# One row operation behind each of eight feed-forward pairs, and an earlier place for the prologue's rows

## The chip, the cores and the metric

The kernel runs on one core of a Trainium2 chip. The metric is the device time of one execution in microseconds. A core has TensorE (PE, the matrix engine; its weight loads are shown apart as PEld), VectorE (DVE), ScalarE (ACT), GpSimd (POOL) and SyncE (SP, which here issues almost all DMAs). The engines run side by side and wait for one another by semaphores.

## The reference

One layer of a decoder trunk, on 2048 rows of 1024 values, in float32:

```python
mem_n = rms_norm(mem, mem_norm)
h = rms_norm(x, mix_pre_norm)
z = h @ w_in                       # split into pool, conformer, gated-conv parts
y = concat([pool_mixer(...), conformer_conv(...), short_gated_conv(...)]) @ w_out
x = x + rms_norm(y, mix_post_norm)
h = rms_norm(x, xattn_pre_norm)
y = cross_attention(h, mem_n, wq, wk, wv, wo)      # 4 heads, 256 memory tokens
x = x + rms_norm(y, xattn_post_norm)
h = rms_norm(x, ffn_pre_norm)
u = causal_dwconv(h @ ffn_w_up, ffn_conv_w)        # 3 taps, 5632 channels
gate, val = split(u)
x = x + rms_norm((silu(gate) * val) @ ffn_w_down, ffn_post_norm)
```

`rms_norm(x, g)` is `x * rsqrt(mean(x*x) + 1e-6) * g`, row by row.

## The kernel before

**Tiles and phases.** The rows are worked through in four tiles of 512. Phases follow each other: a prologue (PREP), the mixers for four tiles (MIX_FIRST, MIX twice, MIX_LAST), attention for four tiles (ATT_FIRST, ATTN), the feed-forward for four tiles (FFN). Every operand of a matmul is split into a high and a low part, and each product is three matmuls (lines 1546 to 1548).

**Weight slots.** Weights go through TensorE in slots of 128 x 1024 values, 24 matmuls each. SyncE loads a slot into one of four `raw` buffers, ten slots ahead at most. ScalarE rounds it into the high half of one of four `pair` buffers (`hi`, L676), three slots ahead of TensorE; GpSimd subtracts that from the raw values for the low half (`lo`, L644). The order of ScalarE's instructions is written out by hand: within a slot's step, `hi` for the slot three places on stands in front of the work on this slot's result.

**Banks.** Results of column slots go in turn through four PSUM banks, `colb`. The list of items of a phase (`PREP_ITEMS`, and `PREP_HIS` for the part that is rounded) gives each item its bank by its place, so an item waits until the item four places before it has been read out. ScalarE writes the rounded value (L685), VectorE the low part (L1093, or L1095 with a gain), and the latter frees the bank.

**Prologue.** TensorE transposes the memory rows (8 items), multiplies them with eight slots for the keys and eight for the values (256 columns per matmul), transposes the pooling maps (`bd`), waits for `h_ready`, and transposes the scaled rows of the first tile, two of eight items behind each of the last four value slots. Between memory transposes and the first key slot stands `banks_ready`, which waits for all. ScalarE sums the squares of the rows; VectorE computes the inverse root `rh` in pieces between the key roundings and scales the four row blocks `xh` (`first_row`, L1132) behind the first four values. Then six convolution slots follow, whose results VectorE uses in three 31-tap convolutions (L1238), and two pooled slots. SyncE stores keys and values to DRAM and, at the end of the prologue, loads the keys of head 0 back (`load_head`).

**First mixer tile.** TensorE needs these keys in `a_rows(0)`. Later it waits for VectorE with the transposes of the next rows: for `h_ready`, and for banks that VectorE frees in `sconv_chunk` (L1307).

**Feed-forward.** A tile has two halves. Each half runs 22 column slots, that is 11 pairs of a gate and a value slot, and 11 row slots into `accb`. For pair j, ScalarE issues `hi` of slot 2j+3, copies the result of slot 2j (L995), issues `hi` of slot 2j+4 and copies slot 2j+1. VectorE (`ffn_pair`) fetches two columns of the halo (L1384), multiplies by the taps (L1393 twice, L1396 four times), stores the halo (L1399); ScalarE does the silu (L998); VectorE multiplies (L1401); ScalarE rounds (L1000); VectorE subtracts (L1201), and that ends the pair. With the end of a pair, ScalarE comes to `hi` of slot 2j+5.

**End of a tile.** `new_rows` adds the normed result to the rows of x: for each of four row blocks a multiply by root and gain (L1176, 1024 columns) and an addition (L1179, the last one L1183). At the last attention tile and the feed-forward tiles but the last, it is interleaved with the first pairs of the next tile by `between`. `LEAD = RB` (4) says how many pairs are done there; the loop over the rest starts at that number:

```python
for r in range(RB):
    if between is not None and r:
        between(r - 1)
    step(nc.vector.scalar_tensor_tensor(y[:, r, :], ..., gain[:, :], ...))
    if r:
        settle(1)
        nc.vector.tensor_tensor(xt[:, r - 1, :], ..., ALU.add)
```

With the last addition x is new (`x_new`). SyncE waits for that at place `ROWS_AT` of its loop over a tile's slots, stores the rows, loads the gain, and two places on the next rows `xt`. ScalarE waits for it before it writes the next result of the row slots.

## Time and profile before

| | |
|---|---|
| median of three timed runs | 2629.49 us |
| the three runs | 2623.81, 2632.18, 2629.49 us |
| the profiled execution | 2624.15 us |
| its span, first to last instruction | 2622.0 us |
| mean granted TensorE clock | 0.989 |

| engine | busy us | share |
|---|---|---|
| TensorE (PE) | 2541.6 | 97% |
| weight loads (PEld) | 2113.0 | 81% |
| VectorE (DVE) | 1514.3 | 58% |
| ScalarE (ACT) | 915.7 | 35% |
| GpSimd (POOL) | 846.1 | 32% |

A row of the timeline has the start in us from the span's start, the duration in us, engine, line, operation, output and input by the program's names, and a count where consecutive instructions were merged; in brackets stands the engine's idle time before the row and what ended it. Matmuls are pipelined, so their rows overlap: the distance from start to start is the pace. The granted clock of 1.00 is TensorE at full speed.

### The profile page before, as it was taken

What the parts mean: (1) busy time and instruction counts of PE and PEld (TensorE: products, weight loads), DVE (VectorE), ACT (ScalarE), POOL (GpSimd) and SP (SyncE); (2) the same over time, 40 slices, a digit from 0 to 9 for tenths busy, and PEclk for the clock granted to TensorE, in tenths of its full rate; (3) what the DMA queues carried; (4) which work ended last, traced back from release to release, by engine and by line L of the source; (5) the groups of instructions that cost most, each with busy time, mean ns of one, the idle gap of its engine ahead of it and who ended that gap; (6) DMA issues with size and microseconds to landing.
All of it is one profiled execution on the core that took longest, in us unless ns stands there. A gap on an engine that the chain in (4) does not pass through costs nothing.

```text
span 2622.0 us, 32632 instructions
## 1 busy us (share of the span) xinstructions
PE 2541.6 (97%) x11713; PEld 2113.0 (81%) x11713; DVE 1514.3 (58%) x2452; ACT 915.7 (35%) x1515; POOL 846.1 (32%) x346
## 2 busy tenths in 40 slices
PE   7999899999999999999999999999999999999997
PEld 6787788878787888887888878888878888878886
DVE  5698877877744532557436276256385264672462
ACT  4433322233334333333333333333334233333332
POOL 6431200000023000034534444444445444445342
PEclk9999999999999999999999999999999999999999
DMA  8796684856868757744333334323354332353331
GB/s 252 250 336 234 209 310 153 299 202 218 290 238 310 301 212 258 268 147 159 113 88 97 95 115 163 117 82 100 92 163 136 94 91 89 90 168 112 89 96 64
DMA packets 313817, 452.62 MB, mean 173 GB/s; under 512 B 12073, under 2 KB 234558, under 8 KB 292670
## 3 DMA queue, kind: packets, MB, share of 16 engines
q1 hardware_dynamic: 305101, 438.56, 49.3%
q10 hardware_dynamic: 8560, 12.06, 1.4%
q8 instruction: 89, 1.46, 0.2%
q14 instruction: 67, 0.54, 0.1%
HBM read 368.78 MB, written 81.79 MB: 172 GB/s over the span
## 4 chain that ended last, share of the span: by engine, by line
PE 82%; DVE 11%; issue 3%; ACT 2%; DMA 1%; SPq 0%; ACTq 0%; DVEq 0%
PE colb L1546 16%; PE colb L1547 16%; PE colb L1548 16%; PE accb L1546 11%; PE accb L1547 11%; PE accb L1548 11%; PE colb L1583 2%; DVE accb L1238 2%; DVE arena L1384 1%; DVE arena L1396 1%; DVE xt L1179 1%; PE accb L1750 1%; DVE arena L1176 1%; DMA raw<-in_xattn_wq 1%; DMA kept<-pair 0%
## 5 line engine op out<-in xcount | busy, mean ns | idle before, releaser
L644 POOL TENSOR_TENSOR pair<-raw,pair 128x1024 fp32r<-128x1024 f32 x339 | 845.2, 2509 | 1748.2 <-ACT pair L676 1737.8
L1546 PE MATMUL colb<-hT,pair 128*128 128x512 f32 x1952 | 765.2, 392 | 16.8 <-issue 12.7
L1547 PE MATMUL colb<-hT,pair 128*128 128x512 f32 x1952 | 763.0, 391 | 0.0
L1548 PE MATMUL colb<-hT,pair 128*128 128x512 f32 x1952 | 762.7, 391 | 0.0
L676 ACT ACTIVATE pair<-raw 128x1024 fp32r<-128x1024 f32 x339 | 355.5, 1052 | 472.6 <-PE accb L1548 277.7
L1546 PE MATMUL accb<-pair,act 128*128 128x512 f32 x1120 | 440.4, 393 | 11.7 <-issue 4.8
L1546 PEld LDWEIGHTS colb<-hT,pair 128*128 128x128 f32 x1952 | 368.7, 189 | 99.0 <-issue 22.5
L1547 PE MATMUL accb<-pair,act 128*128 128x512 f32 x1120 | 437.8, 391 | 0.0
L1548 PE MATMUL accb<-pair,act 128*128 128x512 f32 x1120 | 437.6, 391 | 0.0
L1548 PEld LDWEIGHTS colb<-hT,pair 128*128 128x128 f32 x1952 | 368.4, 189 | 77.3
L1547 PEld LDWEIGHTS colb<-hT,pair 128*128 128x128 f32 x1952 | 368.4, 189 | 75.5
L1393 DVE TENSOR_SCALAR arena<-arena,par 128x512 f32<-128x512 f32 x176 | 219.2, 1286 | 348.3 <-ACT arena L995 347.2
L1546 PEld LDWEIGHTS accb<-pair,act 128*128 128x128 f32 x1120 | 211.2, 189 | 60.4 <-issue 11.3
L1548 PEld LDWEIGHTS accb<-pair,act 128*128 128x128 f32 x1120 | 211.4, 189 | 44.6
L1547 PEld LDWEIGHTS accb<-pair,act 128*128 128x128 f32 x1120 | 211.5, 189 | 42.8
L998 ACT ACTIVATE arena<-arena 128x512 f32<-128x512 f32 x88 | 55.6, 632 | 544.0 <-DVE arena L1399 544.0
L1396 DVE SCALAR_TENSOR_TENSOR arena<-arena,par 128x512 f32<-128x512 f32 x352 | 240.1, 741 | 0.0
L1238 DVE SCALAR_TENSOR_TENSOR arena<-arena,par 128x512 f32<-128x512 f32 x261 | 184.7, 784 | 0.0
L1201 DVE TENSOR_TENSOR act<-arena,act 128x512 fp32r<-128x512 f32 x120 | 88.4, 737 | 82.5 <-ACT act L1000 61.5
L995 ACT ACTIVATE arena<-colb 128x512 f32<-128x512 f32 x176 | 103.0, 585 | 61.6 <-PE colb L1548 61.5
L1165 DVE TENSOR_TENSOR small<-small 128x4 f32<-128x4 f32 x12 | 2.0, 163 | 192.6 <-ACT junk L697 192.6
L1509 DVE TENSOR_TENSOR arena<-arena,accb 128x512 f32<-128x512 f32 x32 | 21.8, 688 | 135.2 <-PE accb L1548 135.2
(162 smaller groups left out, 2421.4 us busy)
## 6 DMA issues: line engine op xcount, KB each, us to landing
pair<-kept SPq DMA_DIRECT2D x123, 1024.0 KB, 5.0
raw<-in_ffn_w_up SPq DMA_DIRECT2D x176, 512.0 KB, 3.8
raw<-in_ffn_w_down SPq DMA_DIRECT2D x176, 256.0 KB, 2.9
kept<-pair SPq DMA_DIRECT2D x41, 1024.0 KB, 7.0
raw<-in_w_in SPq DMA_DIRECT2D x17, 512.0 KB, 6.7
xh<-in_x SPq DMA_DIRECT2D x4, 2048.0 KB, 15.3
xt<-in_x SPq DMA_DIRECT2D x4, 2048.0 KB, 15.5
x_mixed<-xt SPq DMA_DIRECT2D x4, 2048.0 KB, 11.2
```

What stands on the lines that cost most here:

```text
L644: nc.gpsimd.tensor_tensor(pair[:, b, 1, :], raw[:, r, :], pair[:, b, 0, :].bitcast(F32), ALU.subtract).then_inc(lo_done, 1)
L676: nc.scalar.activation(pair[:, b, 0, :], raw[:, r, :], ACT.Copy).then_inc(hi_done, 1)
L995: nc.scalar.activation(uf[:, j % 2, e, HS:LS], colb[bank_of(FFN, c)][:, :], ACT.Copy)\
L998: nc.scalar.activation(cv[:, 0, :], cv[:, 0, :], ACT.Silu).then_inc(silu_done, 1)
L1201: nc.vector.tensor_tensor(dst, src, hi.bitcast(F32), ALU.subtract).then_inc(lo_written, 1)
L1238: step(nc.vector.scalar_tensor_tensor(total, src, w, sums[k % 2], ALU.mult, ALU.add))
L1393: step(nc.vector.tensor_scalar(cv[:, e, :], u[:, e, k:k + T], w, None, ALU.mult))
L1396: step(nc.vector.scalar_tensor_tensor(cv[:, e, :], u[:, e, k:k + T], w, cv[:, e, :], ALU.mult, ALU.add))
L1546: nc.tensor.matmul(dst, sh, mh, start=first, stop=False)
L1547: nc.tensor.matmul(dst, sh, ml, start=False, stop=False)
L1548: return nc.tensor.matmul(dst, sl, mh, start=False, stop=last)
L1583: ins = nc.tensor.transpose(dst[:, n * P:(n + 1) * P], src, ident[:, :])
```

## The change

In `new_rows` with `between`, eight pairs of the next tile are done instead of four: pair 0, multiply of row block 0, pair 1, addition of row block 0, pair 2, multiply of block 1, and so on, to the addition of block 3 behind pair 7. The multiply that stood ahead of pair 0 stands behind it. `LEAD` becomes 8 and `ROWS_AT` of the feed-forward 14.

In the prologue, the transposes of the pooling maps stand behind the second value slot instead of the fourth, the row transposes behind value slots 4 to 7 instead of 5 to 8 (counted from 1), and the eighth value slot behind them all. ScalarE scales the row blocks, two behind each of the first two values, after a wait for the new semaphore `root_ready`. The first key slot waits for each memory value by itself. SyncE's `load_head(sp, 0, 0)` stands behind the last convolution slot's place in its loop.

```diff
-    PREP_HIS = [("mem", k) for k in range(KD)] + [("k", i) for i in range(KD)] + [("v", i) for i in range(KD // 2)] + [("bd",)] +\
-               sum([[("v", KD // 2 + i), ("row", 2 * i), ("row", 2 * i + 1)] for i in range(KD // 2)], [])
+    V_ROWS = KD // 2 - 1
+    PREP_HIS = [("mem", k) for k in range(KD)] + [("k", i) for i in range(KD)] + [("v", 0), ("v", 1), ("bd",), ("v", 2)] +\
+               sum([[("v", V_ROWS + i), ("row", 2 * i), ("row", 2 * i + 1)] for i in range(KD // 2)], []) + [("v", KD - 1)]
@@ SyncE
+                    elif what == "c" and k == CSLOTS - 1:
+                        sp.wait_ge(kv_stored, 16 * 2 * HEADS)
+                        load_head(sp, 0, 0)
                     elif what == "pooled":
...
                         if k == 1:
-                            sp.wait_ge(kv_stored, 16 * 2 * HEADS)
-                            load_head(sp, 0, 0)
-            ROWS_AT = {MIX_FIRST: 0, MIX: 0, MIX_LAST: 0, ATT_FIRST: 0, ATTN: 0, FFN: 8}
+            ROWS_AT = {MIX_FIRST: 0, MIX: 0, MIX_LAST: 0, ATT_FIRST: 0, ATTN: 0, FFN: 14}
@@ ScalarE
                 key_values(1, i)
-                if i == KD // 2 - 1:
+                if i == 0:
+                    sc.wait_ge(root_ready, 1)
+                if i < 2:
+                    for r in (2 * i, 2 * i + 1):
+                        scaled = nc.scalar.activation(xh[:, r, :], xh[:, r, :], ACT.Copy, scale=rh[:, r:r + 1])
+                if i == 1:
+                    scaled.then_inc(h_ready, 1)
                     sc.wait_ge(xp_full, xp_at(PREP, 0, ("bd",)) + 1)
...
@@ VectorE
-            LEAD = RB
+            LEAD = 2 * RB
...
+            ve.sem_inc(root_ready, 1)
             for i in range(KD):
                 key_values(1, i)
-                if i < RB - 1:
-                    first_row(i)
-                elif i == RB - 1:
-                    first_row(i).then_inc(h_ready, 1)
-                if i == KD // 2 - 1:
+                if i == 1:
                     ve.wait_ge(hi_written, PREP_HIS.index(("bd",)) + 1)
...
+                if between is not None:
+                    for r in range(RB):
+                        between(2 * r)
+                        step(nc.vector.scalar_tensor_tensor(y[:, r, :], y[:, r, :], rs[:, r:r + 1], gain[:, :], ALU.mult, ALU.mult))
+                        between(2 * r + 1)
+                        settle()
+                        last = nc.vector.tensor_tensor(xt[:, r, :], xt[:, r, :], y[:, r, :], ALU.add)
+                    last.then_inc(x_new, 1)
+                    return
@@ TensorE
-            banks_ready(PREP, 0, item[PREP]["mem", 0], KD)
-            for i in range(KD):
+            first = split_ready(PREP, 0, place[PREP]["k", 0])
+            keys = bank_free(PREP, 0, item[PREP]["k", 0])[:, 0:M]
+            for k in range(KD):
+                i = item[PREP]["mem", k]
+                pe.wait_ge(col_free[bank_of(PREP, i)], uses_of(PREP, 0, i) + 1)
+                ins = products(keys, pieces(first, k * P, (k + 1) * P), (memT[:, 0, k, :], memT[:, 1, k, :]), k == 0, k == KD - 1)
+            ins.then_inc(slot_used, 1)
+            for i in range(1, KD):
                 column_slot(PREP, 0, place[PREP]["k", i], item[PREP]["k", i], memT, M)
             for i in range(KD):
                 column_slot(PREP, 0, place[PREP]["v", i], item[PREP]["v", i], memT, M)
-                if i == KD // 2 - 1:
+                if i == 1:
                     pe.wait_ge(maps_in, 16 * NW)
                     transposes(PREP, 0, item[PREP]["bd",], [bd[:, e, :] for e in range(NP_)]).then_inc(xp_full, 1)
+                if i == V_ROWS:
                     pe.wait_ge(h_ready, 2)
-                if i >= KD // 2:
-                    for k in range(2 * (i - KD // 2), 2 * (i - KD // 2) + 2):
+                if V_ROWS <= i < KD - 1:
+                    for k in range(2 * (i - V_ROWS), 2 * (i - V_ROWS) + 2):
                         head(PREP, 0, item[PREP]["row", k], k)
```

ScalarE's and VectorE's loops over the row items follow the same new order.

## Rows read from the trace of the kernel before

**Rows 1.** The page, busy us, share of the span and instructions of each engine.

```profile
PE 2541.6 (97%) x11713; PEld 2113.0 (81%) x11713; DVE 1514.3 (58%) x2452; ACT 915.7 (35%) x1515; POOL 846.1 (32%) x346
```

**Rows 2.** Timeline of TensorE, prologue: start, duration, line, idle before in brackets.

```profile
17.79 0.55 PE L1546 MATMUL colb<-act,pair 128*128 128x256 f32 x1 [2.00 <-DVE act L1095]
...
23.47 0.38 PE L1548 MATMUL colb<-act,pair 128*128 128x256 f32 x1
23.69 0.29 PE L1546 MATMUL colb<-act,pair 128*128 128x256 f32 x1
23.81 0.29 PE L1547 MATMUL colb<-act,pair 128*128 128x256 f32 x1
...
60.52 0.58 PE L1546 MATMUL colb<-act,pair 128*128 128x256 f32 x1 [5.12 <-DVE xh L1132]
...
65.30 1.04 PE L1583 MATMUL colb<-ident,xh 128*128 128x128 f32 x8
...
76.53 1.04 PE L1583 MATMUL colb<-ident,xh 128*128 128x128 f32 x8
...
79.62 0.47 PE L1546 MATMUL colb<-hT,pair 128*128 128x512 f32 x1 [2.05 <-DVE hT L1095]
```

**Rows 3.** Timeline of VectorE, prologue.

```profile
15.80 1.66 DVE L1095 SCALAR_TENSOR_TENSOR act<-colb,par,act 128x256 fp32r<-128x256 f32 x4 [0.83 <-ACT act L685]
...
48.30 2.11 DVE L1076 TENSOR_TENSOR small<-small 128x4 f32<-128x4 f32 x1
50.44 0.16 DVE L1077 SCALAR_TENSOR_TENSOR small<-small 128x4 f32<-128x4 f32 x1
...
51.17 2.77 DVE L1132 TENSOR_SCALAR xh<-xh,small 128x1024 f32<-128x1024 f32 x1
...
56.98 0.74 DVE L1132 TENSOR_SCALAR xh<-xh,small 128x1024 f32<-128x1024 f32 x1
```

**Rows 4.** Timelines of ScalarE and GpSimd, prologue.

```profile
46.85 1.05 ACT L676 ACTIVATE pair<-raw 128x1024 fp32r<-128x1024 f32 x1
...
47.98 2.40 POOL L644 TENSOR_TENSOR pair<-raw,pair 128x1024 fp32r<-128x1024 f32 x1 [0.47 <-ACT pair L676]
```

**Rows 5.** Timeline of TensorE, first mixer tile.

```profile
135.27 0.58 PE L1546 MATMUL accb<-act 128*128 128x256 f32 x1 [4.38 <-DMA act<-kvd]
...
211.20 0.95 PE L1583 MATMUL colb<-ident,xh 128*128 128x128 f32 x4 [1.96 <-DVE arena L1307]
```

**Rows 6.** Timeline of VectorE, first mixer tile.

```profile
210.45 0.69 DVE L1307 TENSOR_TENSOR arena<-arena,colb 128x512 f32<-128x512 f32 x1
```

**Rows 7.** Timeline of VectorE, first multiply of the first and fourth boundary.

```profile
1147.55 3.37 DVE L1176 SCALAR_TENSOR_TENSOR arena<-arena,small,gain 128x1024 f32<-128x1024 f32 x1
...
2254.72 1.29 DVE L1176 SCALAR_TENSOR_TENSOR arena<-arena,small,gain 128x1024 f32<-128x1024 f32 x1 [0.21 <-DVE small L1078]
```

**Rows 8.** Timeline of TensorE, third boundary: slots 9, 11 and 25 of the tile.

```profile
1925.02 0.47 PE L1546 MATMUL colb<-hT,pair 128*128 128x512 f32 x1 [0.85 <-issue]
...
1938.28 0.52 PE L1546 MATMUL colb<-hT,pair 128*128 128x512 f32 x1 [2.13 <-issue]
...
2016.65 0.47 PE L1546 MATMUL accb<-pair,act 128*128 128x512 f32 x1
```

**Rows 9.** Windows: stretch, its length, busy us by engine, clock, DMA share, GB/s.

```profile
1938.28:1949.16 10.88, 10.88 (x41) 8.85 (x42) 7.19 (x11) 4.13 (x6) 4.26 (x2) 0.84 0.34 97
```

**Rows 10.** Timeline of VectorE, third boundary: ends of pairs 0, 3, 4, 10.

```profile
1894.06 0.69 DVE L1201 TENSOR_TENSOR act<-arena,act 128x512 fp32r<-128x512 f32 x1 [0.70 <-ACT act L1000]
...
1922.60 3.40 DVE L1179 TENSOR_TENSOR xt<-xt,arena 128x1024 f32<-128x1024 f32 x1
...
1934.14 0.69 DVE L1201 TENSOR_TENSOR act<-arena,act 128x512 fp32r<-128x512 f32 x1 [0.70 <-ACT act L1000]
...
1946.13 0.69 DVE L1201 TENSOR_TENSOR act<-arena,act 128x512 fp32r<-128x512 f32 x1 [0.70 <-ACT act L1000]
...
2013.10 0.69 DVE L1201 TENSOR_TENSOR act<-arena,act 128x512 fp32r<-128x512 f32 x1 [0.70 <-ACT act L1000]
```

**Rows 11.** Timeline of GpSimd, third boundary, same time as the addition at 1922.60.

```profile
1921.79 3.13 POOL L644 TENSOR_TENSOR pair<-raw,pair 128x1024 fp32r<-128x1024 f32 x1 [6.88 <-ACT pair L676]
```

More of the change, by code:

```diff
@@ L1155, in _ @@
                     ins.then_inc(col_free[b], 1)
[L1156 to L1157 removed]
+                if V_ROWS <= i < KD - 1:
+                    for k in range(2 * (i - V_ROWS), 2 * (i - V_ROWS) + 2):
                         lo_item(PREP, 0, PREP_HIS.index(("row", k)), item[PREP]["row", k], hT[:, 1, k, :], hT[:, 0, k, :],
@@ L1172, in new_rows @@
                 ve.wait_ge(xt_in, step_tile.at(p, t, 1) * 16)
+                if between is not None:
[7 more added lines that the diff above has]
+                    return
                 for r in range(RB):
-                    if between is not None and r:
-                        between(r - 1)
                     step(nc.vector.scalar_tensor_tensor(y[:, r, :], y[:, r, :], rs[:, r:r + 1], gain[:, :], ALU.mult, ALU.mult))
@@ L1179, in new_rows @@
                         nc.vector.tensor_tensor(xt[:, r - 1, :], xt[:, r - 1, :], y[:, r - 1, :], ALU.add)
-                if between is not None:
-                    between(RB - 1)
                 settle()
```

9 lines of the change are left out of this document (3 added, 6 removed).

## The prediction

> **What bounds the kernel now.** I read the page's busy table first [rows 1]: TensorE is busy for 97% of the span, VectorE for 58%. So only what takes an idle or slow stretch away from TensorE can shorten the run. Then I listed TensorE's idle stretches in order of time and kept those that the diff can touch.
>
> Prologue [rows 2]: the first key slot starts at 17.79, right behind the eight memory transposes, because it waits for all eight roundings. At 60.52 TensorE has idled 5.12 us for the scaled rows of x, and the slot behind it takes 4.8 us, until the transposes at 65.30, where its neighbours take 2.7: it runs mostly at the lower of the clock's two levels (1.2 and 2.4 GHz); at 79.62 it idles another 2.05 us for the last transposed value's rounding. In the first mixer tile it idles 4.38 us at 135.27 for the keys' load and 1.96 us at 211.20 for VectorE [rows 5].
>
> Feed-forward: at the start of each of four tiles TensorE idles about 2.1 us (2.13 at 1938.28, the others alike) and then runs slow; the mean granted clock of the two slots behind it is 0.84 [rows 8, 9]. What holds it is a ring of three engines. VectorE ends a pair with the subtraction on L1201; only then does ScalarE round the weights of the slot five places on, GpSimd takes their low part, and TensorE may start. The slot at 1938.28 starts 4.14 us behind the subtraction at 1934.14; with no row operation between, the slot at 2016.65 starts 3.55 us behind 2013.10 [rows 8, 10]. That last pair, the eleventh, matters most: the slot that it releases starts as soon as it can, so TensorE has no reserve left there. The pace of the ring over eleven pairs, not the size of one idle stretch, decides how long a tile's first half takes.
>
> **Part by part. The first key slot.** Its 24 products now wait value by value. They share a bank with the fifth memory value, whose rounding is the first of the four that VectorE starts at 15.80 [rows 3]; four took 1.66 us, so the bank is free at about 16.3 instead of 17.79: 1.45 us sooner. The matmuls there start 0.21 us apart, and 0.12 us apart once the clock has risen, at 23.69 [rows 2]. If the rise stays where it is, 1.45 us of work moves into the slow stretch and 1.45 x 0.12/0.21 = 0.8 us is left. I take 1.2, bounds 0.8 and 1.5.
>
> **Scaled rows and transposes.** On VectorE the four row scalings start at 51.17 and take up to 2.77 us, the shortest 0.74 [rows 3]; they are interleaved with value roundings. The long ones overlap GpSimd's operations. ScalarE needs 1.05 us for 1024 columns, as its rounding at 46.85 shows [rows 4], and never has such a long one. ScalarE now waits for the root first. The root's last round was late because of GpSimd: the weights that ScalarE rounds at 46.85 set GpSimd going at 47.98, and VectorE's small multiply at 48.30 took 2.11 us instead of 0.16 [rows 3, 4]. In the new order these weights stand behind that wait, so this collision goes and the root is ready at about 49.0. Four scalings with one weight rounding and one value rounding between them: 49.0 + 4 x 1.05 + 1.05 + 0.4 = 54.7. TensorE, which now does the transposes of the pooling maps after the second value, ends the fourth at about 55.5. The wait of 5.12 is gone with 0.8 us to spare, and its clock loss with it, 4.8 less 2.7 (3.75 from one start of transposes to the next, less 1.04 for the transposes [rows 2]), so 2.1. The eighth value slot now covers the rounding of the last rows, which took the 2.05. Sum 5.12 + 2.1 + 2.05 = 9.2; I take 9.0, as two banks come free only just in time. Queued behind ScalarE's wait are the weights of the fifth value and the rounding of the second; both have over 3 us. If the root comes at 50.8 as before, the rows end 1.8 us later, 1.0 us too late, and the banks of the maps and of the third value, freed behind them, add 0.6 and 0.7 and a little more in the next slot: about 3 us lost, so the lower bound is 6.1.
>
> The Trainium skill speaks against this move: "ScalarE: Activation LUTs", Rules for kernel authors, says that multiplications belong on VectorE, not ScalarE. By it four scalings cost 4 x (1.05 - 0.74) = 1.2 us more, a little over the reserve worked out above, and the wait would stay with 0.4 us. The durations of up to 2.77 us in [rows 3] show why I do not follow it here.
>
> **The keys' load on SyncE's queue** moves in front of one weight load, one stored slot and four stores of pooled rows, all of which are issued one DMA's issue time later. That removes the 4.38 us at 135.27. I cost it at nothing: from the last convolution slot on, VectorE is busy with hardly a gap until L1307 at 210.45, and TensorE waits for exactly that at 211.20 [rows 5, 6]. TensorE only arrives there earlier. Hence also: what the prologue saves up to the last convolution slot moves this whole VectorE chain, and reaches 211. Bounds 0 and 2, since VectorE has two short idles of its own.
>
> **Row operations.** Before, four rounds hold two row operations each, then (after the first pair) 1894.06 to 1934.14 is three rounds of 13.36 us, the next, with one last addition, takes 11.99, and the six up to 2013.10 take 11.16 [rows 10]; TensorE needs 10.88 (48 matmuls of 0.2267). The single row operation costs 0.83, because VectorE idles about 2.25 us in a bare round anyway and only GpSimd is held back. The second costs 1.37 more: the addition at 1922.60 took 3.40 us, waiting for GpSimd's 3.13 us subtraction [rows 10, 11]. After: eight rounds with one. Half hold an addition (11.99), half the multiply, 0.06 us longer (12.05): 96.2, and two bare ones 22.3, together 118.5. Before: 40.1 + 12.0 + 67.0 = 119.1. So each boundary gains 0.5. The idle stretches do change: instead of one of 2.1 with a slow clock, some five of up to 1.1. The slow clock cost nothing in the end, since TensorE caught up with the ring by the eleventh pair; so its going brings nothing. At two of the four boundaries the first multiply stands on the path ahead of pair 0: at 1147.55 it ends the wait for GpSimd, at 2254.72 nothing else is late [rows 7]; there pair 0 starts about 1.1 and 1.0 sooner. At the other two VectorE waits some 4 us for the slot itself. Sum 4 x 0.5 + 2.1 = 4.1. Bounds: if the multiply does not hold GpSimd back, its rounds take 11.5, and four boundaries gain 4 x 4 x 0.55 = 9 more; if each row operation costs half of what two do, (13.36 - 11.16)/2 = 1.1, eight rounds are 98.1 and a boundary loses 1.3, which with the two earlier starts makes 2.1 - 5.2 = -3.
>
> A rule of the Trainium skill on this: "SBUF — State Buffer", Who interferes with whom, says that a VectorE instruction with two SBUF inputs and a GpSimd instruction that reads SBUF exclude each other for the whole instruction. The 3.40 and 3.13 us of [rows 10, 11] agree; without exclusion the multiply's rounds would be the 11.5.
>
> The second store of rows, the gain and the next load of rows move on SyncE from place 8 to place 14. x is new behind pair 7, about 1894 + 7 x 12 + 2.5 = 1980.5; SyncE comes to place 14 when GpSimd has done slot 20, at about 1984. It does not wait, and the weight loads queued behind it have four buffers. Cost nothing.
>
> **Sum.** 1.2 + 9.0 + 0 + 4.1 = 14.3 us. The profiled execution took 2624.15 (span 2622.0), and would take 2609.9. The three timed runs have a median of 2629.49, 5.3 above it: predicted 2629.5 - 14.3 = 2615.2.
>
> **Rivals.** (a) The root is as late as before: prologue 7.3, total 11.4, 2618. For it: VectorE's other small operations there also take 2.3 us. Against: the colliding GpSimd operation can't start. Chance 0.15. (b) The price of a row operation is 1.1: total 10.2 - 3.1 = 7.1, 2622. Against it stands the 11.99. Chance 0.1. (c) The prologue's gain is lost in the first mixer tile, where transfers are dense: VectorE's chain meets more of GpSimd's operations, each costing 2.3 us, and TensorE's longer idle ahead of 211 keeps the clock low longer. Half the 10.2 goes, total 9 or less, about 2622. Chance 0.15. (d) Slower: with 1.1 us of idle in each of five slot pairs, the clock falls to 1.2 GHz in the feed-forward start. A fall for nine matmuls costs 1.8 us and is swallowed by the next idle stretches. It decides the result once it lasts for a whole pair, 48 x 0.2 = 9.6 us less 1.1 of idle, 34 us over four tiles: 2649. For it: behind 2.1 us the clock fell. Against: behind the 0.85 us at 1925.02 it did not [rows 8]. Chance 0.04. (e) The multiply does not hold GpSimd back: 23 saved, 2606. Chance 0.08. (f) The load move does not do what it is for, its transfer being slowed by its neighbours: same time as forecast, since it is off the path.
>
> **Chances.** Forecast 0.48, the others as given. The range 2606 to 2623 takes in (a), (b), (c) and (e) and leaves out (d) and the ends of the rest. Measurement tells about 0.3%, 7.9 us. Faster: the forecast, (a), (e) and a third of (b) and (c), less a little for the scatter of the medians: 0.75. Same 0.21, slower 0.04.
>
> **What would show it.** Right: no idle of TensorE over 1 us between the fourth value slot and the first convolution slot, which starts near 69; VectorE's chain unbroken until the heads of the first mixer tile, TensorE idling there 5 us or more; first feed-forward rounds 12.0 apart on L1201, eight of them, the eleventh subtraction within 1 us of its old distance from the first. Wrong: rounds of 12.3 or 11.5; scaled rows later than the fourth value slot; a granted clock near 0.5 for more than 4 us in the feed-forward start.

## The result and the profile after

The changed kernel took 2610.64 us in the median of four runs (2609.72 to 2612.18), the kernel before 2630.08 (2623.81 to 2632.18) beside it: ratio 0.9932, interval 0.9914 to 0.9951. The profiled execution went from 2624.15 us to 2610.44, its span from 2622.0 to 2608.6, its mean granted clock from 0.989 to 0.995. Both medians and spans count here: the spans, which the steps below are read from, are 13.4 us apart, the medians 19.4, because the profiled execution of before was among its fastest.

The page of the changed kernel: busy time of the engines, which answers [rows 1].

```profile
PE 2532.9 (97%) x11713; PEld 2102.9 (81%) x11713; DVE 1534.2 (59%) x2448; ACT 919.9 (35%) x1519; POOL 841.4 (32%) x346
```

TensorE is 8.7 us less busy with the same matmuls: fewer of them ran at the lower clock. VectorE is busier although four scalings left it: an operation that is held up by GpSimd counts as busy, as a copy of 2.37 us further down shows.

TensorE's timeline of the changed kernel, prologue (start, duration, engine, line, operation; in brackets the idle time before and what ended it). It answers [rows 2].

```profile
16.75 0.55 PE L1554 MATMUL colb<-act,pair 128*128 128x256 f32 x1 [0.76 <-DVE act L1104]
...
53.57 1.06 PE L1591 MATMUL colb<-ident,xh 128*128 128x128 f32 x8
55.10 0.36 PE L1554 MATMUL colb<-act,pair 128*128 128x256 f32 x1 [0.47 <-DVE act L1102]
...
66.32 0.36 PE L1554 MATMUL colb<-act,pair 128*128 128x256 f32 x1
...
69.26 0.40 PE L1554 MATMUL colb<-hT,pair 128*128 128x512 f32 x1
...
105.84 0.47 PE L1554 MATMUL colb<-hT,pair 128*128 128x512 f32 x1 [1.03 <-POOL pair L647]
```

The idle stretches of 5.12 and 2.05 us are gone, the value slots run at the higher clock throughout, and the first convolution slot starts at 69.26. ScalarE and VectorE of the same stretch show why, against [rows 3, 4]:

```profile
47.03 0.17 DVE L1087 SCALAR_TENSOR_TENSOR small<-small 128x4 f32<-128x4 f32 x1
```

```profile
47.28 2.19 ACT L744 ACTIVATE xh<-xh,small 128x1024 f32<-128x1024 f32 x2 [1.98 <-DVEq L1147]
49.38 1.04 ACT L679 ACTIVATE pair<-raw 128x1024 fp32r<-128x1024 f32 x1
50.33 0.36 ACT L688 ACTIVATE act<-colb 128x256 fp32r<-128x256 f32 x1
50.59 2.18 ACT L744 ACTIVATE xh<-xh,small 128x1024 f32<-128x1024 f32 x2
```

The root is ready at 47.2 (its last small operation takes 0.17 us; one took 2.11 before), and two scalings take 2.19 us, so the rows are ready at 52.8, before the transposes behind the fourth value slot start at 53.57.

In the first mixer tile TensorE's waits, which answer [rows 5], are:

```profile
114.95 0.66 PE L1591 MATMUL colb<-ident,pair 128*128 128x128 f32 x4 [2.06 <-ACT arena L838]
152.47 1.53 PE L1717 MATMUL accb<-ident,arena 128*128 128x128 f32 x12 [1.93 <-DVE arena L1249]
182.32 0.47 PE L1554 MATMUL colb<-hT,pair 128*128 128x512 f32 x1 [1.11 <-DVE arena L1300]
189.67 0.47 PE L1554 MATMUL accb<-pair,act 128*128 128x512 f32 x1 [1.64 <-POOL pair L647]
199.06 0.66 PE L1591 MATMUL colb<-ident,xh 128*128 128x128 f32 x4 [1.96 <-DVE arena L1315]
```

And at the start of the first attention tile TensorE waits longer than before, and the clock falls behind it. The first row is that of the kernel before, the second that of the changed one. The window's columns are the stretch, its length, the busy time of PE, PEld, DVE, ACT and POOL, then the granted clock, the DMA share and GB/s.

```profile
822.60 1.97 PE L1750 MATMUL accb<-ident,xh 128*128 128x128 f32 x16 [1.93 <-DVE xh L1084]
```

```profile
809.63 3.62 PE L1766 MATMUL accb<-ident,xh 128*128 128x128 f32 x16 [4.07 <-DVE xh L1093]
```

```profile
809.63:813.63 4.00, 4.00 (x19) 3.92 (x20) 1.98 (x3) 2.41 (x4) 0.00 (x0) 0.57 0.88 364
```

VectorE's timeline at the start of a feed-forward tile, around pair 0 (answers [rows 7, 10]; L1209 is the subtraction that ends a pair, L1179 the multiply, L1182 the addition, L1392 a copy of 128x4):

```profile
1144.56 0.69 DVE L1209 TENSOR_TENSOR act<-arena,act 128x512 fp32r<-128x512 f32 x1 [0.70 <-ACT act L1009]
1145.17 1.27 DVE L1179 SCALAR_TENSOR_TENSOR arena<-arena,small,gain 128x1024 f32<-128x1024 f32 x1
1146.36 2.37 DVE L1392 COPY arena<-arena 128x4 f32<-128x4 f32 x1
...
1156.68 0.69 DVE L1209 TENSOR_TENSOR act<-arena,act 128x512 fp32r<-128x512 f32 x1 [0.70 <-ACT act L1009]
1157.29 1.22 DVE L1182 TENSOR_TENSOR xt<-xt,arena 128x1024 f32<-128x1024 f32 x1
```

A round with a row operation takes 12.12 us (multiply, as here from 1144.56 to 1156.68) or 12.05 (addition), a bare one, without such an operation, 11.16. The row operation itself is short. It pushes the 128x4 copy behind it against GpSimd's subtraction, and the copy stands 2.37 us. In a bare round VectorE waits 2.15 us for ScalarE at about that place, so most of the copy's time costs the round nothing.

At this boundary TensorE idles four times for about 0.9 us, where it idled twice for 2.29 and 2.21 before (at 1188.10 and 1201.45). The clock over the whole stretch is 1.00; before it was 0.98 over the like stretch from 1177 to 1257, and 0.84 over the 10.88 us of [rows 9] at the third boundary:

```profile
1197.13 0.47 PE L1554 MATMUL colb<-hT,pair 128*128 128x512 f32 x1 [0.96 <-issue]
1209.17 0.47 PE L1554 MATMUL colb<-hT,pair 128*128 128x512 f32 x1 [0.89 <-issue]
1221.27 0.47 PE L1554 MATMUL colb<-hT,pair 128*128 128x512 f32 x1 [0.94 <-issue]
1233.31 0.47 PE L1554 MATMUL colb<-hT,pair 128*128 128x512 f32 x1 [0.91 <-issue]
```

```profile
1165.00:1245.00 80.00, 76.08 (x331) 61.23 (x329) 67.01 (x75) 28.92 (x42) 35.54 (x14) 1.00 0.37 113
```

**Where the 13.4 us lie**, as the lead of the changed kernel's trace over the one before at the same place:

| place | lead, us | what came or went |
|---|---|---|
| first mixer slot (116.26 to 105.84) | 10.42 | prologue |
| heads of the first mixer tile (211.20 to 199.06) | 12.14 | VectorE's chain there is 1.7 shorter |
| first attention tile (822.60 to 809.63) | 12.97 | mixer tiles |
| pair 0 of the first feed-forward tile (1156.96 to 1144.56) | 12.40 | clock fall in the attention -1.7, earlier pair 0 +1.1 |
| its 11th pair (1276.26 to 1263.53) | 12.73 | rounds of the first boundary |
| pair 0 of the fourth and last tile (2261.94 to 2248.61) | 13.33 | second earlier pair 0, +0.9 |
| last pair (2558.21 to 2544.80) | 13.41 | |

The table compares one trace of each kernel, and not all of a lead is the change's. In two traces of the kernel before the first mixer slot starts at 116.26 and 115.17, in two of the changed kernel at 105.84 and 103.83: the prologue's gain lies between 9.3 and 12.4 us. From there to the attention the two traces of the changed kernel take 703.8 and 710.2 us, so the 2.55 us that the lead gains in the mixer tiles can't be given to the change.

### The profile page after: what moved, and what is told of

It is laid out like the page before. It is cut to its first block, busy times and chain, and to the rows that moved or that the text cites. A ratio compares the mean times of both kernels' runs of the same rounds, so it can differ in the third digit from the quotient of the medians.

```text
span 2608.6 us, 32631 instructions
## 1 busy us (share of the span) xinstructions
PE 2532.9 (97%) x11713; PEld 2102.9 (81%) x11713; DVE 1534.2 (59%) x2448; ACT 919.9 (35%) x1519; POOL 841.4 (32%) x346
## 4 chain that ended last, share of the span: by engine, by line
PE 90%; DVE 5%; issue 1%; DMA 1%; ACT 1%; SPq 0%; ACTq 0%; DVEq 0%
PE colb L1554 19%; PE colb L1556 18%; PE colb L1555 18%; PE accb L1554 11%; PE accb L1556 11%; PE accb L1555 11%; PE colb L1591 2%; DVE accb L1246 2%; PE accb L1766 1%; DMA raw<-in_xattn_wq 1%; DMA kept<-pair 0%; ACT junk L700 0%; DVE small L1086 0%; DVE small L1087 0%; DVE xh L1093 0%
## 5 line engine op out<-in xcount | busy, mean ns | idle before, releaser
L1401 DVE TENSOR_SCALAR arena<-arena,par 128x512 f32<-128x512 f32 x176 | 238.9, 1397 | 317.2 <-ACT arena L1004 315.2
L1209 DVE TENSOR_TENSOR act<-arena,act 128x512 fp32r<-128x512 f32 x120 | 87.6, 730 | 81.0 <-ACT act L1009 61.5
```

Of the source, the lines that this page charges most:

```text
L1209: nc.vector.tensor_tensor(dst, src, hi.bitcast(F32), ALU.subtract).then_inc(lo_written, 1)
L1401: step(nc.vector.tensor_scalar(cv[:, e, :], u[:, e, k:k + T], w, None, ALU.mult))
```

## The experiments

The line numbers of a kernel are its own. Spans in brackets are those of the profiled execution. The three groups of runs had medians of 2626.8, 2628.7 and 2627.5 us for the kernel before beside them; each ratio is to its own group.

### The unchanged kernel, traced again

> The kernel before, unchanged, for a second trace of it. Ratio 1.000. Theory A: a span and stage times within 1 us of the first trace. Theory B: a span 5 us longer than the first one's 2622.0, the extra in the feed-forward starts, and a mean granted clock under 0.989.

2627.46 us (2619.85 to 2632.11, 12 runs), ratio 1.0003, interval 0.9991 to 1.0016; [2621.5]. From pair 0 of the first feed-forward tile to the last pair it took 1401.30 us, the first trace 1401.25. The feed-forward part of these two traces is the same to 0.1 us; they differ ahead of it, by 1.1 us at the first mixer slot.

### The feed-forward part alone

Against the changed kernel:

```diff
-    V_ROWS = KD // 2 - 1
-    PREP_HIS = ... ("v", 0), ("v", 1), ("bd",), ("v", 2)] + ...
+    PREP_HIS = ... [("v", i) for i in range(KD // 2)] + [("bd",)] + ...
...
-                        scaled = nc.scalar.activation(xh[:, r, :], xh[:, r, :], ACT.Copy, scale=rh[:, r:r + 1])
...
-            first = split_ready(PREP, 0, place[PREP]["k", 0])
+            banks_ready(PREP, 0, item[PREP]["mem", 0], KD)
```

The prologue is the one of before, whole, and so is the place of the keys' load.

> The kernel before with the feed-forward part of the change alone (eight pairs, one row operation behind each, rows stored at place 14). Theory A, the ring of three engines sets the pace to the eleventh pair: eight rounds of 12.1 and two of 11.2 us, TensorE at the eleventh pair within 0.3 us of before in every tile but the two that start earlier, so 2 us faster, about 2628 where the kernel before has 2630. Theory B, the idle stretches of 2.1 us cost more in ordinary executions than in the profiled one of the kernel before, through the clock: 7 us faster, about 2623, with the spread of the runs under 3 us. No fall of the granted clock behind idles of 0.9 us either way.

2624.78 us (2616.77 to 2629.74, 11 runs), ratio 0.9993, interval 0.9982 to 1.0003; [2614.6]. From pair 0 to the last pair 1399.88, that is 1.4 less than before, where eight rounds of one row operation were to give 0.5 at each of four boundaries and the earlier start at the last one 1.0. With the 1.1 us of the earlier first pair 0 the part is worth some 2.5 us of 2627 by the traces; the medians say 2, with an interval that takes in nothing. Of its start the trace shows something else. Row of the unchanged kernel, traced again:

```profile
822.05 1.97 PE L1750 MATMUL accb<-ident,xh 128*128 128x128 f32 x16 [2.15 <-DVE xh L1084]
```

and of this kernel, with its window:

```profile
816.06 2.39 PE L1755 MATMUL accb<-ident,xh 128*128 128x128 f32 x16 [2.16 <-DVE xh L1084]
```

```profile
816.06:820.06 4.00, 4.00 (x21) 3.61 (x22) 2.58 (x4) 3.30 (x5) 2.16 (x1) 0.67 0.99 405
```

A wait of 2.15 us once left the clock at 1.00, and one of 2.16 once brought it down. From the start of these transposes to pair 0 this kernel takes 334.90 us, the kernel before 334.36 in both traces; with the earlier pair 0 it should be 1.1 less, so some 1.6 us are lost. This kernel stood 6.0 us ahead of the unchanged one at this place, with the same instructions before it: that is the size of the scatter between two traces, and it lies in the mixer tiles.

### The prologue alone

```diff
-            ROWS_AT = {..., FFN: 14}
+            ROWS_AT = {..., FFN: 8}
...
-            LEAD = 2 * RB
+            LEAD = RB
...
-                        between(2 * r)
...
-                        between(2 * r + 1)
+                    if between is not None and r:
+                        between(r - 1)
```

> The change with its feed-forward part undone. Theory A: all of the change but 2 us, 17 us faster in the medians, about 2613. Theory B: 12 us faster, about 2618, with the same wide spread of runs as the kernel before (8 us), and the slow stretches behind the 2.1 us idles in its trace longer than 9 matmuls. Both: first convolution slot at about 69.2 us, TensorE's wait for VectorE in the first mixer tile at about 199.

2618.24 us (2607.30 to 2619.31, 9 runs), ratio 0.9957, interval 0.9941 to 0.9972; [2611.3]. Its first mixer slot starts at 105.84, as in the changed kernel. At the attention it stands within 0.3 us of it (809.90), pair 0 comes 336.02 us behind that, against 334.93 in the changed kernel, and the feed-forward part takes 1401.63. So the prologue carries most of the gain, and the earlier pair 0 of the first feed-forward tile is worth the 1.1 us forecast: VectorE has a multiply of 3.37 us ahead of pair 0 here (start 1136.51), and in the changed kernel the 128x4 copy in its place takes 2.32 (1136.28), both held up by GpSimd.

The two parts multiply to 0.9950, the whole has 0.9932; the traces give 2.5 us between this kernel and the changed one (1.1 ahead of pair 0, 1.4 behind it), the medians 5 to 8. The time is Theory B's, and the spread of 12 us wider than its 8, but its sign is not there: the slow stretch behind the 2.26 us idle in this trace is seven matmuls long. What the untraced runs did is not seen, so that difference stays open.

### The changed kernel, traced again

> The changed kernel, unchanged, for more runs beside those of the kernel before, since the feed-forward part alone gave 0.07% and the prologue part alone 0.43%, together 0.50, and the whole change 0.68%. If the parts add up: a ratio of 0.9950, some 13 us. If they do not: 0.993 again, some 18 us, and the spread of the kernel with the prologue's part alone (12 us) gone when both are there.

2612.86 us (2609.39 to 2615.81, 6 runs), ratio 0.9936, interval 0.9921 to 0.9951; [2612.6]. The whole change again, not the sum of the parts. Its prologue is 2.0 us faster than that of the first trace (first mixer slot at 103.83). The matmuls of its first key slot start 0.12 us apart from 16.91 on, those of the first trace 0.21 apart until 21.3, the pace of the lower clock. (The profile's granted clock reads 1.00 there in both traces. That the pace of 0.21 is the lower level's is read from the second trace of the kernel before, which has the same pace with a granted clock of 0.50 from 20 to 22 us.) The lead is lost again in a mixer tile:

```profile
275.81 0.77 PE L1554 MATMUL accb<-pair,act 128*128 128x512 f32 x1 [4.22 <-POOL pair L647]
```

Three more traces with such a start wait 4.20 to 4.24 us at this place, a fourth 5.84. The feed-forward part takes 1400.02, the first trace 1400.24.

### The first key slot waits for all eight values

```diff
-            for k in range(KD):
-                i = item[PREP]["mem", k]
-                pe.wait_ge(col_free[bank_of(PREP, i)], uses_of(PREP, 0, i) + 1)
-                ins = products(keys, ...)
...
-            for i in range(1, KD):
+            banks_ready(PREP, 0, item[PREP]["mem", 0], KD)
+            for i in range(KD):
```

> The changed kernel with the first key slot waiting for all eight memory values again. Forecast: first key slot 0.8 to 1.5 us later than at 16.75, first slot of the mixers 0.8 to 1.5 us later than at 105.8 and 103.8 (the two traces of the changed kernel), in the time as much, which three rounds hardly tell from nothing: 2612 to 2613. If the clock's rise follows the work: the whole 1.5.

2616.84 us (2611.43 to 2618.89, 5 runs), ratio 0.9960, interval 0.9945 to 0.9974; [2609.6].

```profile
18.01 0.36 PE L1554 MATMUL colb<-act,pair 128*128 128x256 f32 x1 [2.19 <-DVE act L1104]
```

The slot starts 1.26 us later than in the changed kernel, and the first mixer slot is at 106.61, 0.8 behind the changed kernel's first trace and 2.8 behind its second. The forecast's 1.2 lies between. But the wait seems to matter for the clock too: of the nine traces of kernels that wait value by value, five have the faster pace from 16.9 us on; of the four that wait for all eight (before twice, the feed-forward part alone, and this one) none has it, and their slot starts behind an idle stretch of 2.0 to 2.3 us instead of 0.7 to 1.1. The median missed its forecast of 2612 to 2613 by 4 us, 4 to 6 behind the changed kernel's. So 0.8 us is what the earlier start gives against a trace with the same pace; how much more it gives by the faster one, a single trace of this kernel does not show.

### The row scalings on VectorE again

```diff
-                if i == 0:
-                    sc.wait_ge(root_ready, 1)
...
-                        scaled = nc.scalar.activation(xh[:, r, :], xh[:, r, :], ACT.Copy, scale=rh[:, r:r + 1])
...
+                        scaled = nc.vector.tensor_scalar(xh[:, r, :], xh[:, r, :], rh[:, r:r + 1], None, ALU.mult)
```

> The changed kernel with the four row scalings on VectorE again, two behind each of the first two values, all else as changed. By the forecast, VectorE's scalings meet GpSimd's subtractions and take up to 2.8 us: rows ready 3 to 5 us later than the fourth value slot's end at 53.1, TensorE idle 3 to 5 us there and slow behind it, first convolution slot at 73 to 76 instead of 69.2, 4 to 7 us slower than the changed kernel (2615 to 2618). By the rival, that a multiplication belongs on VectorE: 4 x 0.3 us sooner, no idle, 2611 or less.

2615.73 us (2613.63 to 2616.74, 4 runs), ratio 0.9947, interval 0.9929 to 0.9965; [2614.6].

```profile
49.83 3.56 DVE L1145 TENSOR_SCALAR xh<-xh,small 128x1024 f32<-128x1024 f32 x2
53.31 0.41 DVE L1096 TENSOR_TENSOR act<-colb,act 128x256 fp32r<-128x256 f32 x1
53.64 3.17 DVE L1145 TENSOR_SCALAR xh<-xh,small 128x1024 f32<-128x1024 f32 x2
```

```profile
56.87 1.17 PE L1588 MATMUL colb<-ident,xh 128*128 128x128 f32 x8 [2.83 <-DVE xh L1145]
```

The four scalings take 6.7 us on VectorE, which shares the stretch with GpSimd, and 4.4 on ScalarE; the rows are ready at 56.8 instead of 52.8, TensorE idles 2.83 us, and the first mixer slot comes 2.7 us later than in the changed kernel (108.55). The first convolution slot starts at 71.98, sooner than the 73 to 76 expected. The root, too, is late again: one of its small operations takes 2.10 us at 46.96. The Trainium skill's rule ("ScalarE: Activation LUTs", Rules for kernel authors: multiplications belong on VectorE) holds for the operation taken alone, 0.74 us in [rows 3] against 1.05 in [rows 4]; here the measurement decides against it, by 3 to 5 us.

### The keys' load behind the stores again

```diff
-                    elif what == "c" and k == CSLOTS - 1:
-                        sp.wait_ge(kv_stored, 16 * 2 * HEADS)
-                        load_head(sp, 0, 0)
...
                         if k == 1:
+                            sp.wait_ge(kv_stored, 16 * 2 * HEADS)
+                            load_head(sp, 0, 0)
```

> The change with the load of head 0's keys put back behind the last pooled rows. If that load is off the path, as forecast: TensorE idles some 4.4 us for it near 125, comes to the heads of the first mixer tile with under 1 us to spare, and starts them at 199 plus or minus 1: time as the change, 2611. If the extra 1.7 us that the change gained between the first mixer slot (10.4) and those heads (12.1) came from TensorE being ahead: heads at 201, 2613.

2610.62 us (2608.95 to 2614.01, 4 runs), ratio 0.9937, interval 0.9916 to 0.9959; [2609.3]: the changed kernel's time.

```profile
122.77 0.58 PE L1553 MATMUL accb<-act 128*128 128x256 f32 x1 [4.41 <-DMA act<-kvd]
196.93 0.66 PE L1590 MATMUL colb<-ident,xh 128*128 128x128 f32 x4 [1.67 <-DVE arena L1314]
```

A wait of 4.41 us comes back and costs nothing. The heads start at 196.93, not at 199, only because this trace had the faster start of its clock (first mixer slot at 103.73, not 105.84): counted from that slot they start at 93.20, in the changed kernel at 93.22. Between these two rows TensorE has no other idle stretch over 0.4 us. In the changed kernel, without the load's wait, it idles 1.93, 1.11 and 1.64 us there, and both reach the heads when VectorE does: a wait that VectorE's chain hides is only passed on.

### Both copies ahead of the weights' rounding

```diff
-                            hi(FFN, t, i + AHEAD)
                             slot_full(sc, FFN, t, i)
                             nc.scalar.activation(uf[:, j % 2, e, HS:LS], ...)
...
+                        for e in range(2):
+                            hi(FFN, t, q * 3 * GF + 2 * j + e + AHEAD)
```

> The changed kernel, ScalarE's order within a pair turned: it first copies both slot results for VectorE and rounds the two weight slots behind that. Theory C, VectorE waits in the ring for ScalarE's second copy: a bare round 10.1 us instead of 11.16, one with a row operation 10.9, no idles in the feed-forward starts, 15 us faster than the changed kernel. Theory D, the ring is the sum of what VectorE and GpSimd may not do at the same time (in a bare round two subtractions of 2.4 on GpSimd, about 5 us of two-input and copy operations on VectorE, and 1.4 us of waits for ScalarE make 11.2): rounds of 11.2 and 12.1 to 12.6 as before, time within 5 us of the changed kernel, rather slower because weights come 1 us later.

2644.40 us (2641.78 to 2646.63, 4 runs), ratio 1.0060, interval 1.0041 to 1.0079; [2641.3]. Rounds of 12.12 with a row operation and 11.25 bare: VectorE's wait for ScalarE's copy falls from 2.15 us to 0.36 in a bare round, and the pace does not get better. Instead its operations stand beside GpSimd's:

```profile
1163.10 5.14 DVE L1402 TENSOR_SCALAR arena<-arena,par 128x512 f32<-128x512 f32 x2
```

```profile
1163.02 4.93 POOL L647 TENSOR_TENSOR pair<-raw,pair 128x1024 fp32r<-128x1024 f32 x2 [7.19 <-ACT pair L679]
```

Two scalings that take 0.88 us together when GpSimd is quiet took 5.14. The edit does a second thing: the weights are rounded behind the copies, so GpSimd starts 1.97 us behind the start of a pair's last subtraction, and not 1.00. So the kernel shows that the wait for the copy alone does not set the pace, and not more. It lost some 32 us against the changed one, far more than either theory had: TensorE idles some 0.95 us at six pairs of a first half and 1.4 to 1.7 at another, and in the second halves it is held to the ring's 11.25 us, where the changed kernel's runs at its own 10.88.

### GpSimd's low parts halved

```diff
+                c = 512 if p == FFN else 1024
-                nc.gpsimd.tensor_tensor(pair[:, b, 1, :], raw[:, r, :], ...)
+                nc.gpsimd.tensor_tensor(pair[:, b, 1, 0:c], raw[:, r, 0:c], ...)
```

The low parts of half of the feed-forward weights' columns are left out.

> The changed kernel with GpSimd's subtraction in the feed-forward done on 512 of the 1024 columns; the low parts of the other half are left out. That takes 1.2 us off each of the two subtractions in a round. Theory D, the ring is the sum of what VectorE and GpSimd exclude each other from: rounds of 12.1 become 9.7, so TensorE's pace of 10.9 takes over, none of its idles of 0.9 us is left, about 5 us gained per tile, 2591. Its rival, that the ring is VectorE's and ScalarE's own work and GpSimd's only meets it by chance: rounds within 0.5 of 12.1 and idles of 0.9.

2590.45 us in a single run [2588.6]. The pairs' ends are 10.88 us apart from the first round on, with row operations between, which is TensorE's own need, and TensorE has no idle stretch of 0.2 us there. Both the pace and the time are Theory D's.

```profile
1144.70 3.29 POOL L648 TENSOR_TENSOR pair<-raw,pair 128x512 fp32r<-128x512 f32 x2 [7.09 <-ACT pair L680]
```

### All row operations behind the eleventh pair

```diff
-            ROWS_AT = {..., FFN: 14}
+            ROWS_AT = {..., FFN: 22}
-            LEAD = 2 * RB
+            LEAD = GF
...
                 if between is not None:
+                    for n in range(GF):
+                        between(n)
```

> The changed kernel with all eleven pairs of the first half done before any of the eight row operations, which then stand together behind the eleventh pair; rows are stored at place 22. Theory A, the ring's pace up to the eleventh pair decides: ten bare rounds of 11.16 us are 111.6 where the changed kernel has 119.0; TensorE needs 108.8 and has some 4 us in hand, so it does not idle at all in the first eleven pairs, and each of the four tiles gains 5.5 us: 22 us faster than the changed kernel, about 2589. Theory B, the idles cost through the clock alone, which the change has removed already: no faster than the changed kernel, 2611, or slower, since the next result of the row slots then waits for the old rows (8 operations, 10 us, in the way of row slot 6): up to 4 x 5 us slower.

2619.91 us (2615.83 to 2622.28, 7 runs), ratio 0.9963, interval 0.9950 to 0.9976; [2618.9]. Ten bare rounds take 111.6 us (1148.92 to 1260.53; 112.0 to 112.4 in the other tiles), and TensorE does not idle in them: Theory A's pace held, its time missed by 31 us. The row operations come all at once, each against GpSimd, and the next result needs the old rows out of its place, as the last part of Theory B had it:

```profile
1272.38 3.41 DVE L1183 TENSOR_TENSOR xt<-xt,arena 128x1024 f32<-128x1024 f32 x1
```

```profile
1284.23 0.80 PE L1548 MATMUL accb<-pair,act 128*128 128x512 f32 x1 [5.06 <-ACT arena L1027]
```

The wait of 5.06 us (4.12 to 4.86 in the other tiles), and a clock of 0.50 to 0.65 over the 4 us behind it, take back more than the 2.7 to 3.9 us that TensorE idled in a first half of the changed kernel: the feed-forward part takes 1406.17 us instead of 1400.24. Moving work out of the ring pays only if it fits before its reader.

### Three operations ahead of the last pairs, five behind

```diff
+        row_taken = sem("row_taken")
...
+                                    if half == 0 and r < RB - 1:
+                                        sc.wait_ge(row_taken, t * (RB - 1) + r + 1)
+                                    elif half == 0:
                                         sc.wait_ge(x_new, step_tile.at(FFN, t, 1))
...
+                    for n in range(GF):
+                        between(n)
+                        if n == GF - 4:
+                            times(0)
+                        elif n == GF - 3:
+                            settle()
+                            plus(0).then_inc(row_taken, 1)
+                        elif n == GF - 2:
+                            times(1)
+                    times(2)
+                    settle(1)
+                    plus(1).then_inc(row_taken, 1)
...
```

`LEAD` and `ROWS_AT` are 11 and 22 as in the last one, and a row block's place is freed on its own.

> The changed kernel with the row operations later but not last: one behind each of the eighth, ninth and tenth pairs, five behind the eleventh; and ScalarE's copy of a row block's next result waits for that block's rows alone, by a new semaphore. Theory A (the ring decides up to the eleventh pair, and behind it only the old rows hold the next result): rounds of 11.16 seven times, then three of 12.1, idles of about 1.5 us in the ninth to eleventh pair, no more than 1 us of idle where the kernel with all operations last had 5.06; 3 to 4 us gained per tile over the changed kernel, about 2597. Theory E, that any order of these eight operations costs the same in the end, since GpSimd's subtractions are in their way wherever they stand (3.4 us each): 2611, as the changed kernel.

2599.16 us (2593.92 to 2600.84, 4 runs), ratio 0.9886, interval 0.9867 to 0.9906; [2598.9]. This is 11 to 14 us faster than the changed kernel. Seven rounds of 11.16 are followed by three of 12.11, 12.07 and 12.10; TensorE idles twice at the end of the first half:

```profile
1255.03 0.47 PE L1572 MATMUL accb<-pair,act 128*128 128x512 f32 x1 [0.82 <-POOL pair L648]
1267.14 0.47 PE L1572 MATMUL accb<-pair,act 128*128 128x512 f32 x1 [0.96 <-POOL pair L648]
```

From pair 0 of the first feed-forward tile to the last pair 1386.7 us, against 1400.2 in the changed kernel: 13.5 us, 3.4 for a boundary, where five row operations out of the ring at 0.9 each would be 4.5.

## Why the prediction was right, and where not

**What bounds.** Right: TensorE is the bound, and only its idle and slow stretches moved the time. The forecast of 14.3 us for the profiled execution stands against 13.7 (2624.15 to 2610.44), 2609.9 against 2610.44. The steps behind it did less well than the sum, and that it came out to 0.6 us is luck: 2.55 us gained in the mixer tiles and 1.7 lost in the attention were not in it, the row operations gave 2 us less, and two traces of one kernel differ by more than that.

**Prologue.** 10.2 forecast, 10.42 measured in this pair of traces, 9.3 to 12.4 over two traces of each kernel. By its parts: the root was forecast at 49.0 and came at 47.2; the rows at 54.7, and came at 52.8; the fourth value slot at 55.5, and ended at 53.5, since with the scalings off VectorE and no clock fall every slot ahead of it ran sooner, so the reserve was 0.7 us, where 0.8 was forecast. The first convolution slot was to start near 69: 69.26. The first key slot started 1.04 us sooner, not 1.45: the four roundings start at 16.00 and not at 15.80, and the slot starts 0.27 us behind the end of the first. The forecast took the clock's rise as fixed; it is not, and the pace in this slot alone moves the end of the prologue by 2 us. Rival (a), the late root, is refuted: GpSimd's operation starts at 50.5, behind the root. And the wait for the rows that the kernel with scalings on VectorE shows (2.83) is what the move to ScalarE took away. What the new order of transposes and value slots is worth by itself was not run.

**Keys' load.** Forecast nothing, measured nothing: ratios 0.9937 and 0.9932. The size of the wait at the heads, "5 us or more", was wrong: it is 1.96. TensorE spent its head start at four earlier waits (2.06, 1.93, 1.11, 1.64; of these 1.29 stood at the first place before, and 0.97 at the last); the added 4.5 us are the load's 4.38. The end of VectorE's chain was the right thing to look at, the place of the wait was not. VectorE's chain itself became 1.7 us shorter than before, which no step foresaw. Its cause stays open. From the first mixer slot to the heads it is 94.94 and 94.81 us in the two traces of the kernel before, and 92.9 to 93.8 in all ten traces with a new prologue; but it was 92.57 in the kernel with the feed-forward part alone, whose instructions up to there are those of before.

**First attention tile.** This step was missing. TensorE arrives there early, waits 4.07 us instead of 1.93, the clock falls to 0.57 and 16 transposes take 3.62 us instead of 1.97. It costs 1.7 us: from there to pair 0 the kernel with the prologue alone takes 336.02 us, the one before 334.36 in both traces. The second trace of the changed kernel and the one with the prologue alone (4.26 and 4.37 us of wait) show the same slow transposes. This is what rival (c) described, at another place and at a third of its size.

**Row operations.** This is the term that was mis-sized: 4.1 forecast, about 2.1 measured. The two earlier starts gave 1.1 and 0.9, as forecast (1.1 and 1.0). The rounds took 12.12 and 12.05 us where 12.05 and 11.99 were forecast: 0.06 to 0.07 us each, in eight rounds of four boundaries some 2.1 us in all, so that a boundary gained 0.05 to 0.3 instead of 0.5. The reading behind it held. The last addition of before (11.99) was a good row to take the price from: 0.96 for a multiply and 0.89 for an addition, against 0.89 and 0.83. Rivals (b) with 1.1 and (e) with nothing for a multiply are both refuted. But a term that is the small difference of large numbers (118.5 against 119.1) needs its rounds to 0.05 us, and they came from one row of each kind.

That the slow clock cost nothing in the end is right as well: it is gone (1.00 over the 47 us from 1934 at the third boundary, in place of 0.84), and the eleventh pair is no sooner for it than the rounds explain. Rival (d) is refuted: four idle stretches of 0.9 us did not bring the clock down.

**Medians.** Taking the profiled execution's distance from the median, 5.3 us, over to the other kernel was the weaker half of the last step: the changed kernel's profiled execution lies at its median (2610.44 and 2610.64), and in its second trace above it (2614.60 and 2612.86). The forecast of 2615.2 missed by 4.6 us, nearly all of it this.

**The ring.** The forecast said that only GpSimd is held back by a row operation and that one costs 0.83; the reason was argued, not shown. The trace of the kernel with all row operations last lets one follow a bare round once around the ring:

```profile
1204.59 1.04 ACT L679 ACTIVATE pair<-raw 128x1024 fp32r<-128x1024 f32 x1
```

```profile
1205.72 4.93 POOL L647 TENSOR_TENSOR pair<-raw,pair 128x1024 fp32r<-128x1024 f32 x2 [6.22 <-ACT pair L679]
```

```profile
1210.86 2.73 DVE L1398 SCALAR_TENSOR_TENSOR arena<-arena,par 128x512 f32<-128x512 f32 x4
```

ScalarE rounds the weights (1.13 us to GpSimd's start), GpSimd does its two subtractions (4.93), VectorE the taps and the halo, which it reaches only when GpSimd is done (3.17), and then ScalarE's silu, VectorE's multiply and ScalarE's rounding follow (1.93): 11.16. In a round with a row operation GpSimd's two take 5.42 to 5.48 instead of 4.93 (they start at 1206.01 and 1193.91 in the changed kernel), and the taps start some 0.4 us later behind them. So GpSimd is held back as forecast, and that is about half of the price.

Three kernels bear on it. Giving VectorE its input sooner did not make the rounds shorter (11.25 against 11.16), though GpSimd started 1 us later there; halving GpSimd's work brought them to TensorE's 10.88 even with row operations, in one run; taking the row operations out gave 11.16. So the pace of a round is what GpSimd and VectorE need one after the other, with ScalarE's short steps between. That agrees for VectorE's additions (3.41 us at 1272.38 beside GpSimd, 1.22 at 1157.29) with the Trainium skill ("SBUF — State Buffer", Who interferes with whom: the two engines exclude each other for a whole instruction where VectorE has two SBUF inputs and GpSimd reads SBUF). The copies and scalings of the ring have one input, and the traces show them waiting as well (2.37 and 5.14 us). Spreading eight row operations over eight rounds instead of four gained 0.3 us at the first boundary and under 0.1 at the others: nothing of itself. Only putting them where the ring isn't the bound gains, as the last experiment shows.

## What to carry to other kernels

Where two engines shut each other out, count the pace of a loop as the sum of their stretches and of what stands between them, and gain by moving work out of the loop, not by spreading it within. But check who reads what the moved work frees, because the reader may then have to wait (5.06 us here, until the places were freed one by one). Taking away a wait gains nothing where the next reader waits for another engine's chain anyway (4.4 us here); and a head start is spent at the first place where TensorE waits for something else, sometimes with a clock fall on top.

## What the hardware showed that was not expected

- Scaling 128x1024 on ScalarE took 1.1 us each in pairs (2.19), on VectorE beside GpSimd 1.6 to 1.8 (3.17 and 3.56 for two), although VectorE alone took 0.74.
- Even a 128x4 copy on VectorE stood 2.37 us while GpSimd was at work, and 0.16 us otherwise. How long an operation stands says nothing of its size here, and not what it costs either: a round with such a copy and a row operation was only 0.9 to 1.0 us longer.
- The granted clock fell behind an idle stretch of 2.16 us in one trace and not behind 2.15 at the same place in another; at the heads of the first mixer tile it was 0.57 behind 1.96 us before and 1.00 behind 1.96 in the changed kernel. Behind the 3.97 to 4.59 us at the attention it fell in all ten traces that had such a wait; behind the 0.9 us of the feed-forward starts it never fell.
- In the first key slot the pace changed from 0.21 to 0.12 us at 21.3 us in one trace of the changed kernel and was 0.12 from 16.9 on in another, which is worth 2 us at the first mixer slot.
- The traces of each unchanged kernel agree to 0.3 us over the 1400 us of the feed-forward part, but the two of the changed kernel differ by 6.4 us between the first mixer slot and the attention. A step of 2 us there can't be read from one trace.
